# Cross attention with tokens on the partitions, in 512-column units, and two-head stick values

## The reference

```
h   = rmsnorm(x, g_mix);  z = h @ w_in        # sb_q, sb_k, sb_v, ml_..., x_q, gates
kv  = rmsnorm(mem, g_mem) @ w_mem_kv          # mem_k, mem_v
y_x = softmax(rms(x_q_h, gq) . rms(mem_k_h, gk)^T / 16) @ mem_v_h     # for each head h of 4
y_sb = stick_breaking(sb_q, sb_k, sb_v)       # 8 heads of width 128, two at a time
y_ml = mlstm(...)
x = x + (g0 * (y_sb @ w_sb) + g1 * (y_ml @ w_ml) + g2 * (y_x @ w_x)) @ w_out;  x = x + mlp(x)
```

## Time and profile before

| | us |
|---|---|
| median of 3 runs | 1178.87 (1178.81 to 1178.95) |
| profiled execution, its own time | 1178.82 |
| its span, first to last instruction | 1177.0 |
| PE busy / DVE busy / ACT busy | 1168.5 / 821.0 / 666.8 |
| first product with weights | 10.37 |
| end of the last `stick_sums`, in the mlstm stage | 197.80 |

### The profile page before, as it was taken

One profiled execution on the slowest core, in us unless ns is written; L12 is line 12 of the kernel. 1 busy time (PEld: TensorE's weight loads), 2 busy tenths in 40 slices (PEclk: granted clock), 3 DMA queues, 4 the chain that ended last, 5 costly groups with the idle time before them and its releaser, 6 DMA issues.

```text
span 1177.0 us, 17884 instructions
## 1 busy us (share of the span) xinstructions
PE 1168.5 (99%) x7562; PEld 1061.0 (90%) x7562; DVE 821.0 (70%) x956; ACT 666.8 (57%) x783; POOL 15.6 (1%) x34
## 2 busy tenths in 40 slices
...
GB/s 326 170 159 128 144 144 148 164 169 198 200 221 189 202 156 157 199 181 226 168 213 161 214 133 193 181 173 193 164 185 244 191 167 161 168 182 188 221 206 38
DMA packets 181135, 212.60 MB, mean 181 GB/s; under 512 B 6700, under 2 KB 147376, under 8 KB 181056
## 3 DMA queue, kind: packets, MB, share of 16 engines
...
...
## 4 chain that ended last, share of the span: by engine, by line
PE 87%; DVE 9%; ACT 3%; issue 1%; DMA 0%; DVEq 0%; ACTq 0%
PE ps L242 27%; PE ps L2139 20%; PE ps L356 13%; PE ps L2502 7%; PE ps L361 7%; PE ps L1864 5%; PE ps L2096 4%; DVE w_lo L210 3%; DVE arena L1354 3%; PE ps L1913 1%; PE ps L1867 1%; ACT w_hi L204 1%; DVE arena L1690 1%; PE ps L2446 1%; DMA pcol<-in_params 0%
## 5 line engine op out<-in xcount | busy, mean ns | idle before, releaser
L210 DVE TENSOR_TENSOR w_lo<-raw,w_hi 128x2048 fp32r<-128x2048 f32 x187 | 427.9, 2290 | 194.9 <-ACT w_hi L204 194.5
L204 ACT CAST w_hi<-raw 128x2048 fp32r<-128x2048 f32 x187 | 355.5, 1904 | 190.5 <-PE ps L2139 102.2
L242 PE MATMUL ps<-x_both,w_hi 128*128 128x256 f32 x2080 | 383.5, 286 | 0.0
L242 PEld LDWEIGHTS ps<-x_both,w_hi 128*128 128x128 f32 x2080 | 325.0, 191 | 4.4 <-issue 2.8
L242 PE MATMUL ps<-x_both,w_lo 128*128 128x256 f32 x1040 | 294.1, 283 | 0.0
L2139 PE MATMUL ps<-w_hi,x_both 128*128 128x512 f32 x688 | 213.2, 391 | 0.0
L242 PEld LDWEIGHTS ps<-x_both,w_lo 128*128 128x128 f32 x1040 | 199.0, 191 | 0.0
L356 PE MATMUL ps<-x_both,w_hi 128*128 128x512 f32 x656 | 157.3, 392 | 0.0
L2139 PEld LDWEIGHTS ps<-w_hi,x_both 128*128 128x128 f32 x688 | 128.6, 188 | 26.7 <-issue 0.2
L356 PEld LDWEIGHTS ps<-x_both,w_hi 128*128 128x128 f32 x656 | 120.6, 188 | 23.5
L2139 PE MATMUL ps<-w_lo,x_both 128*128 128x512 f32 x344 | 134.0, 389 | 0.0
...
## 6 DMA issues: line engine op xcount, KB each, us to landing
...
```

The costliest lines, as they stand in the source:

```text
L204: nc.scalar.copy(w_hi[:, s], raw[:, s]).then_inc(S(f"w_hi{s}"), 1)
L210: nc.vector.tensor_tensor(w_lo[:, s], raw[:, s], w_hi[:, s].bitcast(FP32), ALU.subtract)\
L242: last = nc.tensor.matmul(dst, l, r, start=start and k == 0 and m == 0, stop=stop and k == nk - 1 and m == 2)
```

## The change

Cross attention is done for two heads at a time. k, q and v of a pair are six wide units (k 0 and 1, q 0 and 1, v 0 and 1) with tokens on the partitions, accumulated in two banks, one for each half of the tokens. The squares are summed along the free axis by ACT (`accum_out`), the inverse norm of k is applied by DVE as a number per partition while it copies k out of PSUM, that of q goes into the scale of the exponential, and the product of the two gains goes into the copy of the turned k. q and k of each head are turned by eight transposes on PE (`cross_turn_in`). Bank 0, 1 and 2 are used by k, q and v in turn, and the waits on them follow `cross_uses`. The opening loads memory and x in halves, each before its first weights, and the first three units in halves; the parameters used first go by a small transfer of their own; the squares of memory and x are folded by DVE and summed by products of one column. Of the stick units, v of two pairs becomes two wide units. The attention steps, the thin gate sums and the splits stand at other places of the three engines' orders.

```
+    (("g_mix", 8), ("g_mem", 8), ("q_norm_g", 2), ("k_norm_g", 2), ("conv_w", 64), ("conv_b", 16), ("g_mlp", 8),
+     ("ml_norm_g", 8), ("norm_mix_pre_w_2", 8)),
     (("conv_w_2", 128),),
-    (("conv_w", 64), ("conv_b", 16), ("g_mix", 8), ("g_mem", 8), ("g_mlp", 8), ("ml_norm_g", 8),
-     ("q_norm_g", 2), ("k_norm_g", 2), ("norm_mix_pre_w_2", 8)),
...
+def cross_unit(p, what, n):
+    return 6 * p + {"k": 0, "q": 2, "v": 4}[what] + n
+def cross_bank(p, what, t):
+    if (p, what, t) == (0, "q", 1):
+        return bank(6, 512)
+    return bank(cross_slot(what, t), 512)
+def cross_slot(what, t):
+    return {"k": (0, 1), "q": (2, 0), "v": (1, 2)}[what][t]
+def cross_uses(p, what, t):
+    return 2 * p + ((what, t) in (("q", 1), ("v", 0), ("v", 1)))
...
+    in_half(memt, a["mem_t"], "mem_in", 0)
+    first_load(0, w_kv, 0, 0)
+    in_half(memt, a["mem_t"], "mem_in", 4)
+    first_load(1, w_kv, 4, 0)
+    in_half(res, a["x_t"], "x_in", 0)
+    first_load(2, w_in, 0, XQ)
+    in_half(res, a["x_t"], "x_in", 4)
+    wide_load(cross_unit(0, "q", 1), w_in, 4, XQ)
+    for n in range(2):
+        wide_load(cross_unit(0, "v", n), w_kv, 4 * n, D)
+    for what, w, at in (("k", w_kv, 0), ("q", w_in, XQ), ("v", w_kv, D)):
+        for n in range(2):
+            wide_load(cross_unit(1, what, n), w, 4 * n, at + 512)
+    for j in (0, 2):
+        load(sp, stick_unit(j, "q"), halves(w_in, 0, j * CW + SBQ))
+        load(sp, stick_unit(j, "k"), halves(w_in, 0, j * CW + SBK))
+        for n in range(2):
+            wide_load(stick_unit(j + n, "v"), w_in, 4 * n, j * CW + SBV)
...
+    def cross_squares(p, what, t):
+        done(p, what, t)
+        if p == 0 and what == "k":
+            act.wait_ge(S("in_pair"), 1)
+        else:
+            act.wait_ge(S("c_ssq"), 4 * p + 2 * "kq".index(what) + t - 1)
+        for h in range(2):
+            last = A(c_junk[:, 2 * t + h], cross_bank(p, what, t)[:, h * CW:(h + 1) * CW], ACT.Square,
+                     accum_out=c_ssq[:, "kq".index(what), t, h:h + 1])
...
+    def cross_v(p, t):
+        done(p, "v", t)
+        A(c_v[:, t], cross_bank(p, "v", t), ACT.Identity, scale=mem_col[:, t:t + 1])\
+            .then_inc(S(f"bank{cross_slot('v', t)}"), 1)
...
+    for u in range(SLOTS):
+        next(ahead)
+    mem_sq = cells(2048, KT, T)
+    mem_high(0)
+    early(0, 0)
+    square(mem_sq, memt, 0)
+    early(0, 2)
+    square(mem_sq, memt, 1)
...
+    square(mem_sq, memt, 3)
+    x_high(0)
+    x_high(1)
+    early(2, 0)
+    early(2, 2)
+    cross_squares(0, "k", 0)
+    x_high(2)
+    x_high(3)
+    cross_squares(0, "k", 1)
+    split()
+    for b in range(4):
+        square(mix, res, b)
+    split()
+    act.wait_ge(S("eps"), 1)
+    act.wait_ge(S("c_e"), 1)
+    inv_rms(mem_col, mem_sums, D)
+    cross_inverse(0, "k")
+    cross_squares(0, "q", 0)
+    cross_squares(0, "q", 1)
+    split()
+    act.wait_ge(S("in_ss"), 2)
...
-            act.wait_ge(S("mem_col"), 1)
-        finished(act, u)
-        for t in range(2):
-            last = A(c_v[:, t], unit_bank(u)[:, t], ACT.Identity, scale=mem_col[:, t:t + 1])
-        last.then_inc(taken(u), 1)
-    def cross_square_k(i):
-        evacuated(act, cross_units(i)[0])
...
+    split()
+    for b in range(4):
+        x_normed(b)
+    cross_squares(1, "q", 0)
+    split()
+    cross_out(1)
+    cross_squares(1, "q", 1)
+    cross_inverse(1, "q")
+    split()
+    cross_k(2)
+    cross_exp(2)
+    cross_v(1, 0)
+    split()
+    cross_v(1, 1)
+    act.wait_ge(S("cst_in"), 16)
+    A(x_hi[:, M0 + 3], cst[:, P:3 * P], ACT.Copy).then_inc(S("sums_r"), 1)
+    split()
+    cross_out(2)
+    cross_k(3)
+    split()
+    cross_exp(3)
+    split()
+    act.wait_ge(S("pcol_rest"), 16)
...
+    def folds(sq, before):
+        dve.wait_ge(S("in_sq"), 4 * before + 4)
+        for n, m in enumerate((4, 2, 1)):
+            need(dve, "in_pair", 3 * before + n)
...
+    folds(cells(2048, KT, T), 0)
+    x_low(2)
+    x_low(3)
+    split()
+    mean_terms(1, mem_sums, e_k, 1.0)
+    folds(mix, 1)
+    split()
+    for t in range(2):
+        cross_k(0, t)
+    for t in range(2):
+        cross_q(0, t)
+    mean_terms(2, x_sums, e_q, float(CW))
+    split()
...
+    for b in range(4):
+        low(H0 + 2 * b, mix[:, 2 * b:2 * b + 2], "xn_hi", b + 1, "xn_lo")
+    cross_q(1, 1)
+    split()
+    cross_turned(2)
+    cross_max(2)
+    split()
+    cross_weights(2)
+    cross_pT(2)
+    split()
+    cross_low(2)
+    evac(stick_unit(0, "q"), s_q)
+    cross_turned(3)
+    split()
+    cross_max(3)
+    evac(stick_unit(0, "k"), s_k)
+    split()
+    cross_weights(3)
+    cross_pT(3)
...
+    gate_inputs()
+    cross_low(3)
+    gate_rows()
...
+    def cross_half(p, what, n, t, hi=None, lo=0):
+        u, at, dst = cross_unit(p, what, n), (YSB if what == "q" else M0) + 4 * n, cross_bank(p, what, t)
+        s = u % SLOTS
+        if n == 0 and (p, what, t) != (0, "q", 1):
+            need(pe, f"bank{cross_slot(what, t)}", cross_uses(p, what, t))
+        for kind, (wt, xt) in enumerate(((w_hi, x_hi), (w_hi, x_lo), (w_lo, x_hi))):
+            for k in range(4):
+                if kind == 1 and p == 0:
+                    pe.wait_ge(S("in_lo"), lo + k // 2 + 1)
+                elif u < SLOTS:
+                    if kind == 0:
+                        hi(k // 2)
+                    half, full = (("w_hi_half", "w_hi"), None, ("w_lo_half", "w_split"))[kind] if kind != 1 else (0, 0)
+                    if kind != 1:
+                        pe.wait_ge(S(half if k < 2 else f"{full}{u}"), u + 1 if k < 2 else 1)
+                elif k == 0 and kind != 1:
+                    pe.wait_ge(S(f"{('w_hi', 0, 'w_split')[kind]}{s}"), u // SLOTS + 1)
+                if kind == 0 and u >= SLOTS and hi is not None:
+                    hi(k // 2)
+                last = nc.tensor.matmul(dst, xt[:, at + k, t * P:(t + 1) * P], wide(wt[:, s])[:, k],
+                                        start=n == 0 and kind == 0 and k == 0, stop=n == 1 and kind == 2 and k == 3)
+        if t == 1:
+            last.then_inc(S(f"unit{s}"), 1)
+        elif n == 1:
+            last.then_inc(S("c_half"), 1)
...
+    def token_sums(sq, n):
+        pe.wait_ge(S("in_pair"), 3 * n)
+        for t in range(2):
+            last = mm(bank(5, 2, 2)[:, n - 1, t:t + 1], sq[:, 0, t * P:(t + 1) * P], ones[:, 0:1])
...
+    def cross_turn_in(h):
+        p, at = h // 2, h % 2 * CW
+        pe.wait_ge(S("bank0"), 2 * p + 2)
+        pe.wait_ge(S("bank1"), 2 * p + 1)
+        pe.wait_ge(S("bank2"), 2 * p + 1)
+        for src, b in ((k_s, 3), (q_s, 7)):
+            for d in range(2):
+                for t in range(2):
+                    last = tr(bank(b, 2, T)[:, d, t * P:(t + 1) * P], src[:, t, at + d * P:at + (d + 1) * P])
+        last.then_inc(S("c_turn"), 1)
...
+    first_unit()
+    cross_whole(0, "k", 1, mem_second, 2)
+    cross_whole(0, "q", 0, x_first, 4)
+    token_sums(cells(2048, KT, T), 1).then_inc(S("in_ss"), 1)
+    cross_whole(0, "q", 1, x_second, 6)
+    cross_half(0, "v", 0, 0)
+    token_sums(mix, 2)
+    mm(bank(4, T), ones, mix[:, 0]).then_inc(S("in_ss"), 1)
+    cross_half(0, "v", 0, 1)
     pe.wait_ge(S("ident"), 16)
-    pe.wait_ge(S("mem_rs"), 1)
...
-    last.then_inc(S(f"unit{q}"), 1)
+    cross_turn_in(0)
+    cross_half(0, "v", 1, 0)
+    pe.wait_ge(S("x_rs"), 1)
+    cross_logits(0)
+    cross_half(0, "v", 1, 1)
+    cross_half(1, "k", 0, 0)
+    cross_turn(0)
+    cross_half(1, "k", 0, 1)
+    cross_values(0)
+    cross_half(1, "k", 1, 0)
+    cross_turn_in(1)
+    cross_half(1, "k", 1, 1)
+    cross_logits(1)
+    cross_whole(1, "q", 0)
+    cross_turn(1)
+    cross_half(1, "q", 1, 0)
+    cross_values(1)
+    cross_half(1, "q", 1, 1)
+    cross_half(1, "v", 0, 0)
+    cross_turn_in(2)
+    cross_half(1, "v", 0, 1)
+    cross_logits(2)
+    cross_whole(1, "v", 1)
+    cross_turn(2)
...
-    pe.wait_ge(S("cst_in"), 16)
-    for i in range(1, 5):
-        k, q, v = (U("cross", i, n, 3) for n in range(3))
-        mem, x = (M0, YSB) if i < 4 else (H0, H0)
-        if i == 4:
-            pe.wait_ge(S("xn_lo"), 4)
-        half(k, 0, mem)
-        cross_sums(i - 1)
-        if i == 4:
-            gate_sums()
-        half(k, 1, mem)
-        half(q, 0, x)
-        cross_logits(i - 1)
-        half(q, 1, x)
-        half(v, 0, mem, TOK)
-        cross_turn(i - 1)
-        half(v, 1, mem, TOK)
-        cross_values(i - 1)
-        if i == 4:
-            gate_columns()
...
+    pe.wait_ge(S("xn_lo"), 4)
+    half(stick_unit(0, "q"), 0, H0)
+    cross_values(2)
+    half(stick_unit(0, "q"), 1, H0)
+    half(stick_unit(0, "k"), 0, H0)
+    cross_turn_in(3)
+    half(stick_unit(0, "k"), 1, H0)
+    cross_logits(3)
+    stick_v(0, 0, 0)
+    stick_v(0, 0, 1)
+    cross_turn(3)
+    gate_sums()
...
+    stick_v(0, 1, 0)
+    cross_values(3)
+    stick_logits(0)
+    stick_v(0, 1, 1)
+    unit(stick_unit(1, "q"), H0)
+    stick_sums(0)
+    gate_columns()
```

(90 more changed lines are left out.)

492 lines of the change are left out of this document (221 added, 271 removed).

## The result

| | median, us | runs | ratio to before |
|---|---|---|---|
| before | 1178.9 | beside each experiment again, 1178.8 to 1178.9 | |
| after | 1190.1 | 1189.9 to 1191.4 (4) | 1.0098, 95% 1.0086 to 1.0110 |

The account below looks back on a forecast made before the run. The prediction took the sum of PE's work to bound the kernel. To 1178.82 us it added -5.6 (PE's work), -3.0 (opening) and +15.3 (eight waits), +6.7 in all, for 1185.5 us; range 1175 to 1190.

Parts of the forecast that it names:

- rival C: PE's clock falls at the new, longer waits, 2.5 us for each slow start, giving 1192 us; chance 0.08.
- (a): Opening, unit 1: the second half of its high weights is late by 0.3 us.
- (c): First v product: PE waits 2.4 us for bank 1, that is, for DVE to scale k.
- (f): cross_turn(2): PE waits 3.1 us for DVE's weights, which stand behind the split of unit 13.
- (g): cross_turn(3): PE waits 2.1 us for DVE's weights, behind a chain of ACT and DVE steps with splits.
- (h): First stick sums: PE waits 2.7 us behind DVE's gate rows, split, stick terms and low part.
- (b): Unit 3: PE waits 1.8 us together, as ACT squares k only after DVE's first fold and DVE's low part follows.
- (d): cross_turn(1): the ACT and DVE chain behind turn_in(1) is late, 1.2 us with the values behind it.
- (e): cross_turn_in(2): PE waits 1.7 us for q's copy on DVE.
- A: Rival: the waits are covered as before, so the change gives its PE gain, 1171 us; chance 0.16.
- B: Rival: each ACT and DVE hop is a tenth shorter, leaving 8.5 us of waits, 1178.7, no change; chance 0.14.
- D: Rival: in the opening the first landings come as late as two halves did, 1187 us; chance 0.08.

Follow-up runs that it names:

- e1_fill: Kernel after, with PE doing unused products of ones in front of four of its waits, so these are filled and not removed; 1185.8 us.
- e10: Kernel before, with PE made to wait for a chain of 10 POOL fills ahead of cross_turn of heads 1, 2 and 3; 1191.3 us.
- e2: Kernel after, with DVE making the cross weights of heads 2 and 3 ahead of the split that stood before each; 1183.3 us.
- e3: Kernel after, with DVE's gate rows moved behind the first stick low part and PE's gate columns half a unit later; 1186.4 us.
- e4: Kernel after, with the split of unit 4 behind k's inverse norm on ACT and behind k's scaling on DVE; 1188.3 us.
- e9: e6 plus two moves: squares of k write to free cells, so ACT skips a fold wait, and x_normed(2) and (3) precede unit 9's split; 1174.7 us.
- e7: Kernel after, with the second half of the memory loaded ahead of the first weights; 1191.0 us.
- e8: Kernel after, with all 192 KB of parameters in the first small transfer instead of 10 KB; 1190.7 us.
- e11: Kernel before, with PE made to wait for 4 POOL fills ahead of cross_turn of heads 1, 2 and 3; 1184.0 us.
- e5: Kernel after with the edits of e2, e3 and e4, and two low parts of the normed x moved behind the copy of turned q(2); 1176.4 us.
- e6: e5 with 22 instead of 14 warm-up products ahead of the first weights; 1176.3 us.

## Why the forecast fell short, point by point

- **The step that failed: the clock.** The sum of the prediction has no term for it; "granted clock 1.00" was among the things that the trace would show. The mechanism was there as rival C, with a chance of 0.08 and a price of 2.5 for each slow start. It came on top of the forecast waits: 6.0 us in the profiled execution. `e1_fill` took the idle time away and the falls behind it went, e10 brought the waits alone and a fall came: shown. The price of 2.5 fits no single fall: one of 3.4 us cost 1.5 or 1.6 and one of 6.8 cost 2.9. It was read from the warm-up products, beside which the granted clock stands at 1.00, so it was not the price of a recorded fall. Without the clock term the found terms give +6.4 where +6.7 was forecast. That is luck in part: the waits were forecast 1.9 too large, and the two gains together 1.6 too large. The low chance rested on the rows of before, which had no wait over 0.7 and so could say nothing of one of 3.
- **The waits** are at the places named but for (a), 13.4 in sum instead of 15.3. The four largest, (c), (f), (g) and (h), are within 0.2 of the forecast; (b), (d) and (e) are 0.5 to 1.4 smaller. In us, forecast and shown idle:

| | (a) | (b) | (c) | (d) | (e) | (f) | (g) | (h) |
|---|---|---|---|---|---|---|---|---|
| forecast | 0.3 | 1.8 | 2.4 | 1.2 | 1.7 | 3.1 | 2.1 | 2.7 |
| found | 0 | 0.4 | 2.4 | 0.7 | 1.0 | 2.9 | 1.9 | 2.6 |

  The causes given for (f) and (g), (h) and (c) are shown by e2, e3 and e4, where one move each took the wait away or most of it. (b) was mis-sized: a square of 256 columns out of PSUM was bounded by the exponential (0.46), and the group of the kernel after shows (count, busy, mean ns, idle before) 376 ns; with the read of its sum it takes 0.36 from start to start (30.33 to 30.69):

```profile
L653 ACT ACTIVATE arena<-ps 128x256 f32<-128x256 f32 x8 | 3.0, 376 | 3.4 <-DVE arena L1306 2.7 <-PE ps L2097 0.7
```

  Four squares stand in that walk, so this is 0.4 of the 1.4. The rest of (b) I didn't separate.
- **PE's work** is 4.5 less, not 5.6. A group of wide products has an edge: after the values of head 0, 12 wide products take 60.80 - 57.87 = 2.93 where 12 x 0.2267 is 2.72, 0.21 more:

```profile
57.87 2.19 PE L2097 MATMUL ps<-w_hi,x_both 128*128 128x512 f32 x8
...
60.80 1.03 PE L2050 MATMUL ps<-cst,arena 128*128 128x128 f32 x8
```

  But the kernel before has such an edge too: 48 narrow products behind the logits take 47.23 - 41.29 = 5.94 where 48 x 0.12 is 5.76, 0.18 more. The wide form adds 0.03 there, too little to be the cause. Nor is it the four products with one moving column (taken at 0.22 each, 0.9): in e9 they take 0.36 and 0.37 a pair (25.06 to 25.42, 33.78 to 34.15), 0.73 in all. Where the 1.1 us went stays open.
- **The opening** came at 8.43 instead of 7.9, within its bounds. DVE's chain, and not PE, sets when the first v can start, 25.8 us after the first product; it moves with the same landings, so the gain in the start is passed on.
- **The loads** of weights, counted at nothing, were late nowhere: no wait of PE or of a split names one behind the opening.
- **The rivals.** A and B (waits covered or a tenth shorter) fall: the waits are there in size. D falls: the start is 2.5 earlier. But A's number is not far from what mended orders reach: 1171 was its time, and e9, with its orders mended, has 1174.7.

The change's two parts thus stand apart: the new tiling with its small work gives 4.5 us and the opening 2.5; the order in which DVE and ACT were left takes 13.4, and the clock makes the damage of the three longest waits larger by three quarters (8.0 shown idle, 6.0 on top).

## What to carry to other kernels

When PE sets the time, walk every new wait with the durations of the other engines: here it gave the four largest to within 0.2 us and named the places of the others. Then price each wait of a size that was followed by a low clock (here 1.9 us and more) with a fall (1.5 us, in one place 2.9), and don't read a clock of 1.00 in a kernel without such waits as evidence about one that has them. Where an engine does both work in bulk (splits, 2.29 us) and short steps that PE waits for, the short step goes ahead of the bulk: such moves, with those in the opening, turned 11.2 us lost into 4.1 gained in `e9_best`. And take what an experiment should give from the same execution that the losses were read from.

## What the chip showed beside it

- Behind the opening, waits of 1.92 to 2.91 us were followed by a fall of the granted clock from 2.4 to 1.2 GHz in 12 of the 15 cases of the profiled executions. The three others are 2.91 in e7 and 2.68 and 2.75 in e10. A low stretch of 3.4 us cost 1.5 or 1.6, and one of 6.8, behind the first `stick_sums`, 2.9. So a kernel with such waits spreads: 3.8 us from its fastest to its slowest run in e3, 0.4 in `e9_best`.
- No wait of 1.86 us or less behind the opening was followed by a fall. The 1.86 stands at `cross_turn(3)` in five profiled executions (the kernel after, e3, e4, e7, e8); of 1.68 there are two cases, in e3 and e8, and of about 1.2 three, in e11. What decides between 1.86 and 1.92, and from one execution to the next, no run here shows.
- There the fall comes after the wait, when PE works again: in the kernel after 0.5 to 1.3 us behind the first product (resumed at 34.24, 98.32 and 143.30, low from 34.8, 99.6 and 144.0), in e10 0.2 behind (97.52, low from 97.7).
- In the opening the clock was low in e1, e2, e3, e5, e7 and e8, where PE had idled for 1.86 to 3.30 us ahead of the first weight product, and not in the kernel after (2.59) and e4 (2.82), nor in e6 and e9, where 22 warm-up products left 0.69 and 0.62. In e2 and e7 it was low before that product started (from 8.2 and 8.4; starts 8.65 and 9.62). The time didn't show it, since another engine's chain was the later one.
